# Routing inside the merge, expert rows by indirect DMA, and projections moved into the attention rounds

## The reference, cut to what matters

```python
def moe_swiglu(h, w_router, b_router, w_gate, w_up, w_down):
    t = h.reshape(n_tok, d)                      # 256 tokens x 1024, h = rmsnorm(x)
    logits = t @ w_router + b_router             # 8 experts
    top_v, top_e = lax.top_k(logits, 2)
    gate = jax.nn.softmax(top_v, axis=-1)
    # every token goes to its two experts
    one = (silu(xb @ w_gate[e]) * (xb @ w_up[e])) @ w_down[e]     # 1024 -> 3584 -> 1024
    y = zeros(n_tok, d).at[row_tok].add(out * row_g)

x = x + moe_swiglu(rmsnorm(x, ffn_norm_g[1]), ...)
x = rmsnorm(x, final_norm_g)                     # end of the first block
z = rms_norm(x, pre_mix_norm) @ w_in             # second block, 11 rwkv columns of 128 (r, k, v: 3 each; lora: 2), q, kv, s5
r, k, v, wl, al, gl = split(token_shift(z_rw, mu))
bonus = sum(r * k * r_k, per head) * v           # added to the rwkv output
```

## Time and profile before

| | |
|---|---|
| runs | 2463.23, 2454.6, 2454.49 us; median 2454.6 |
| profiled execution | 2454.6 us, of it span 2452.6 (2.0 around it) |
| mean granted TensorE clock | 0.97 |
| TensorE busy | 2360.8 us, 96% |
| DVE, ACT, POOL busy | 24%, 13%, 6% |
| read from DRAM | 528.09 MB |
| merge's last matmul to the first matmul of expert 0 | 900.36 to 934.41 us |
| eight experts | 934.4 to about 1849 us |
| second block: project, attend | 1865.70 to 1979.90, 1979.90 to 2064.99 us |

### The profile page before, as it was taken

One profiled execution on the slowest core, in us unless ns is written; L12 is line 12 of the kernel. 1 busy time (PEld: TensorE's weight loads), 2 busy tenths in 40 slices (PEclk: granted clock), 3 DMA queues, 4 the chain that ended last, 5 costly groups with the idle time before them and its releaser, 6 DMA issues. The chain is left out here.

```text
span 2452.6 us, 44903 instructions
## 1 busy us (share of the span) xinstructions
PE 2360.8 (96%) x20471; PEld 1590.4 (65%) x20471; DVE 599.1 (24%) x1351; ACT 313.8 (13%) x646; POOL 143.6 (6%) x205
## 2 busy tenths in 40 slices
PE   8999999999999989999999999999998988989998
PEld 7777788888677774535353534444456866668887
DVE  2432220002432121011010110111014265643334
ACT  0222210000231201000000000000001233110002
POOL 1000100000000103000000000000001153300000
PEclk9999999999999988999999999999999967989999
DMA  8322434336322345999999999999994110065330
GB/s 302 136 72 70 168 138 166 143 104 227 132 74 69 137 172 203 386 368 392 388 414 368 412 366 412 368 404 375 380 378 133 62 70 10 1 222 190 110 118 34
DMA packets 165402, 532.02 MB, mean 217 GB/s; under 512 B 16060, under 2 KB 31326, under 8 KB 148830
## 3 DMA queue, kind: packets, MB, share of 16 engines
q1 hardware_dynamic: 153728, 527.76, 57.1%
q10 hardware_dynamic: 11486, 1.41, 0.4%
HBM read 528.09 MB, written 1.05 MB: 216 GB/s over the span
## 5 line engine op out<-in xcount | busy, mean ns | idle before, releaser
L182 PE MATMUL bank<-hT,ring 128*128 128x256 f32 x2720 | 609.1, 382 | 4.3 <-PEq L826 2.8
L182 PE MATMUL bank<-ring,moe_he 128*32 128x512 f32 (+2 forms) x6144 | 577.0, 537 | 0.4 <-DVE moe_he L2008 0.4
L182 PEld LDWEIGHTS bank<-hT,ring 128*128 128x128 f32 x2720 | 514.5, 191 | 83.5 <-issue 13.1
L182 PEld LDWEIGHTS bank<-ring,moe_he 128*32 128x32 f32 x6144 | 199.2, 110 | 373.2 <-issue 371.4
L182 PE MATMUL bank<-ring,moe_actT 128*32 128x256 f32 x5352 | 291.7, 379 | 0.0
L182 PEld LDWEIGHTS bank<-ring,moe_actT 128*32 128x32 f32 x5352 | 173.8, 110 | 116.7 <-issue 3.4
L2062 DVE TENSOR_TENSOR moe_act<-moe_silu,bank 128x512 f32<-128x512 f32 (+2 forms) x48 | 26.8, 614 | 537.5 <-PE bank L182 537.5
L182 PE MATMUL bank<-ring 128*128 128x256 f32 x384 | 86.0, 386 | 6.8 <-DVE ring L631 6.8
L182 PEld LDWEIGHTS bank<-ring 128*128 128x128 f32 x384 | 73.9, 193 | 17.7 <-issue 7.3
L182 PE MATMUL bank<-cffn_act,ring 128*128 128x256 f32 x352 | 79.7, 379 | 0.4 <-DVE cffn_act L1495 0.4
L182 PE MATMUL bank<-ffn_act,ring 128*128 128x256 f32 x352 | 79.4, 379 | 0.0
(11 more groups left out here) (690 smaller groups left out, 2039.8 us busy)
## 6 DMA issues: line engine op xcount, KB each, us to landing
ring<-in_moe_w_down SPq DMA_DIRECT2D x55, 2048.0 KB, 14.3
ring<-in_moe_w_gate SPq DMA_DIRECT2D x32, 2048.0 KB, 16.3
ring<-in_moe_w_up SPq DMA_DIRECT2D x32, 2048.0 KB, 11.0
ring<-in_w_in SPq DMA_DIRECT2D x29, 2048.0 KB, 8.5
ring<-in_moe_w_gate SPq DMA_DIRECT2D x28, 1536.0 KB, 8.9
ring<-in_moe_w_up SPq DMA_DIRECT2D x28, 1536.0 KB, 8.7
ring<-in_w_up SPq DMA_DIRECT2D x10, 2048.0 KB, 9.8
ring<-in_w_out SPq DMA_DIRECT2D x6, 2048.0 KB, 7.9
```

The lines of the kernel that those rows point to most:

```text
L182: ins = pe.matmul(out, lhsT, rhs, start=start, stop=stop, **kw)
```

## The change

**A, early route.** The blocks of `rmsnorm` and `route` are gone. A new `Router` lives in the ring's spare slot. In `merge` of layer 1, after each pair of tiles DVE writes `hT` = `xT`·g (not yet divided by the norm), ACT squares the pair, and TensorE multiplies `hT` by the router's weights and the squares by a column of ones, 32 columns wide (`sums`, four matmuls for a pair, 16 in all). The four column groups are folded by two matmuls, ACT takes the root, DVE forms the logits, and TensorE turns `hT` (16 transposes). At the start of `experts`: ACT copies the turned rows scaled by the norm, DVE picks the experts, TensorE counts positions and gathers for expert 0 as before; a broadcast of the norm scales `hT` for the later use of it. SP writes the token rows to DRAM (`h_rows`, 1 MB) before it issues the experts' slabs.

**B, rows by DMA.** For the experts 1 to 7 the 24 gather matmuls give way to `locate` (2 matmuls, which give each place its token's number), three small DVE operations and three indirect DMAs on POOL's queue (128 rows of 1 KB each), which fetch the rows that DVE then turns into `moe_he`. For the experts 0 to 6 `moe_ye` is written to DRAM by four DMAs on ACT's queue (96 pieces of 1 KB each) and not scattered; during the last expert POOL fetches each token's two rows (four indirect DMAs of 128 rows of 4 KB), DVE weighs and adds them (`weigh`), TensorE turns the sum (`bring`, 16 transposes) and DVE adds it once. Only expert 7 is scattered.

**C, late tiles.** In `project` the v features and the r·k·r_k sums are gone and the three r features stand one by one behind `up`; DVE's and ACT's work follows. In `attend` the three v features follow rounds 1 to 3, the sums and the first s5 feature round 4, the second s5 feature round 5; v is turned after the last round.

```diff
@@ merge, TensorE @@
+            def sums(q):
+                if q == 0:
+                    pe.wait_ge(m.load_in[3], 16)
+                pe.wait_ge(xg_done.sem, 2 * q + 2)
+                pe.wait_ge(sq_done.sem, q + 1)
+                for k in (2 * q, 2 * q + 1):
+                    for c, w, x in ((k % 4, router.w[:, k, :], m.hT), ((k + 2) % 4, router.count, router.sq)):
...
+                if router and q:
+                    sums(q - 1)
-            m.settle(pe, pair_ready)
+                sums(3)
+                pe.wait_ge(added.sem, 2)
+                for j in range(4):
+                    turn(j)
+                pe.wait_ge(part_out.sem, 1)
+                for t in range(TT):
+                    m.mm(pe, m.bank[1][:, 16 * t:16 * t + 9], part_sums[:, t * P:(t + 1) * P], router.fold[:, 0:9], True, True,
+                         tok_ready if t else None)
+                for j in range(4, 2 * KD):
+                    turn(j)
@@ moe @@
-    rmsnorm(m, m.xT[:], m.hT, "ffn_norm_g", 1)
-        route(m, x)
-        experts(m, x, prep)
+        experts(m, x, prep, Router(m), Routes(m, x, c2))
@@ experts, TensorE, for each e @@
                 contract(e, 0)
-                if e:
-                    scatter(e - 1)
                 if e + 1 < N_EXPERTS:
-                    gather(e + 1)
+                    locate(e + 1)
+                if e == LAST:
+                    bring()
                 pe.wait_ge(at_ready.sem, half * e + half)
                 contract(e, 1)
@@ experts, ACT @@
                     if e >= 2:
-                        act.wait_ge(sc_ready.sem, e - 1)
+                        act.wait_ge(written.sem, 64 * (e - 1))
                     act.activation(x.ye[:, 0:2, :], DN[0][:].rearrange("p (g n) -> p g n", g=2), ACT.Copy).then_inc(ye_ready.sem, 1)
+                    act.wait_ge(ye_ready.sem, 2 * e)
+                    for cg in range(4):
+                        act.dma_start(x.y_rows[(e - 1) * CAP:e * CAP, cg * T:(cg + 1) * T].rearrange("(g r) n -> r g n", r=32),
+                                      x.ye[32 * cg:32 * cg + 32]).then_inc(written.sem, 16)
@@ experts, POOL @@
+            for e in range(1, N_EXPERTS):
+                g.wait_ge(index_ready.sem, e)
+                g.wait_ge(he_ready.sem, e)
+                for j in range(GRP):
+                    g.indirect_dma_start(x.picked[:, j, :], None, x.rows_of_h,
+                                         bass.IndirectOffsetOnAxis(ap=x.index[:, e % 2, j:j + 1], axis=0)).then_inc(picked.sem, 16)
+            g.wait_ge(written.sem, 64 * LAST)
+            for t, j, to in ((0, 0, x.h_tok[:, 0, :]), (0, 1, x.second), (1, 0, x.h_tok[:, 1, :]), (1, 1, x.second)):
+                if t and j:
+                    g.wait_ge(weighed.sem, 1)
+                g.indirect_dma_start(to, None, x.y_rows, bass.IndirectOffsetOnAxis(ap=x.pair_row[:, t, j:j + 1], axis=0))\
+                    .then_inc(brought.sem, 16)
@@ project @@
-    ORDER = (("kv", 5), ("r", 3), ("swap", 3), ("k", 3), ("v", 3), ("norm", 3), ("lora", 2), ("q", 3), ("kw", 4), ("up", 9),
-             ("swap_w", 1), ("gates", 9), ("turned", 3))
+    ORDER = (("kv", 5), ("swap", 3), ("k", 3), ("lora", 2), ("norm", 3), ("q", 3), ("kw", 4), ("up", 9), ("r0", 1),
+             ("swap_w", 1), ("gates", 9), ("r1", 1), ("turned", 3), ("r2", 1))
@@ attend, TensorE, after round n @@
+                        if n <= 4:
+                            pe.wait_ge(x_out.sem, 2 * n)
+                        if n <= 3:
+                            project("v", n - 1, m.bank[6][:, 0:T], late_ready)
+                        elif n <= 5:
+                            if n == 5:
+                                pe.wait_ge(late_out.sem, 4)
+                            else:
+                                for p in range(3):
+                                    o = m.bank[7][:, p * T:(p + 1) * T] if p < 2 else m.bank[6][:, T:2 * T]
+                                    pe.matmul(o, m.pair_ones[:], bonus[:, p, :], start=True, stop=True, skip_group_check=True)
+                            project("s5", n - 4, m.bank[6][:, 0:T], late_ready)
```

More of the change, by code:

```diff
@@ L1294, in _ @@
             k = Engine(v, vchain.sem)
+            if router:
+                k.step(v.tensor_reduce(router.fold, m.ident[:].rearrange("p (c n) -> p n c", c=4), AX.X, ALU.add))
             for h in range(2):
@@ L1544, in __init__ @@
         self.iota = sb("iota", [P, CAP])
+        self.picked = spare[:, 2 * D:2 * D + GRP * T].rearrange("p (g n) -> p g n", g=GRP)
+        self.token = spare[:, 2 * D + GRP * T:3 * D].rearrange("p (t n) -> p t n", t=TT)
+        self.diag, self.part = sb("diag", [P, 32]), sb("part", [P, 1])
+        self.found, self.where = sb("found", [P, GRP, 32]), sb("where", [P, GRP, 1])
+        self.index = sb("index", [P, 2, GRP], mybir.dt.uint32)
+        self.rows_of_h = m.nc.dram_tensor("h_rows", [4 * T, T], F32, kind="Internal").ap()
+        self.y_rows = m.nc.dram_tensor("y_rows", [NO_ROW + 1, D], F32, kind="Internal").ap()
+        self.zero, self.row0 = sb("zero", [P, D // P]), sb("row0", [P, 8])
+        self.key, self.held, self.best = (sb(n, [P, TT, 8]) for n in ("key", "held", "best"))
+        self.pair_g = sb("pair_g", [P, TT, 2])
+        self.pair_row = sb("pair_row", [P, TT, 2], mybir.dt.uint32)
+        self.both = sb("both", [P, TT, 2, 8])
+        self.second = spare[:, 2 * D:3 * D]
         self.slot = sb("slot", [P, GRP])
@@ L1828, in experts @@
+def experts(m, x, prep, router, rt):
     nc = m.nc
@@ L1846, in _, with locate @@
         def _(pe):
+            def locate(e):
+                pe.wait_ge(token_ready.sem, 1)
+                pe.wait_ge(sel_ready.sem, e)
+                for t in range(TT):
+                    m.mm(pe, m.bank[4][:, 0:CAP], x.token[:, t, :], x.sel[:, t, :], t == 0, t == TT - 1,
+                         gath if t == TT - 1 else None)
             def gather(e):
-                if e:
-                    pe.wait_ge(sel_ready.sem, e)
                 for g in range(GRP):
@@ L2267, in _ @@
                     m.done_with_slab()
-                    for j in range(3):
-                        feature("r", j * P)
-                    m.done_with_slab()
                     pe.wait_ge(consts.sem, 1)
@@ L2303, in _ @@
                         single(m.pair_ones[:], t1[:, p, :])
-                    for j in range(2):
-                        feature("lora", j * P)
-                    m.done_with_slab()
                     for j in range(3):
@@ L2329, in _ @@
                     ins.then_inc(s_ready.sem, 1)
+                    feature("r", 0)
                     moved(pe, "kw", 2)
@@ L2333, in _ @@
                         single(gsel[:, j, :], gl)
-                    pe.wait_ge(dot_in.sem, 1)
-                    for p in range(3):
-                        ins = pe.matmul(half(6 + p // 2, p % 2), m.pair_ones[:], t2[:, p, :], start=True, stop=True)
-                    ins.then_inc(dot_ready.sem, 1)
+                    feature("r", P)
                     pe.wait_ge(p_ready.sem, 1)
```

502 lines of the change are left out of this document (324 added, 178 removed).

## The result

The changed kernel takes 2435.5 us (median of 5 runs, 2427.7 to 2437.5) against 2454.5 before (5 runs, 2447.3 to 2463.2): ratio 0.990, 95% interval 0.988 to 0.993. The forecast was 2399 with a range of 2388 to 2424. The direction was right, the size was not: 19 us of 56.

A forecast was written before the change was run, and what follows sets the result against it. TensorE, busy for 96% of the span, was taken as the bound, with the DMA engines' weight stream close behind in the experts. 2454.6 - 18.2 (A) - 34.0 (B) - 3.6 (C) = 2398.8, said as 2399 us, range 2388 to 2424.

The forecast's parts named there:

- A: Out-projection's end to first expert: 34.05 us go and 15.9 come back, giving -18.2 us, between -15 and -20.5.
- B, TensorE's side: Experts: scatters and gathers leave TensorE, `locate` and 16 transposes come; -34.0 us if nothing new is waited for.
- B, the new wait: Experts, second contract wave: three row fetches take 11 us of the 13 left, so they fit with 2 to spare.
- The first rival: Experts: fetched rows come later than 13 us, TensorE waits 2 to 3 us in each of 7 experts; 2415, chance 0.22.
- B, DMA's side: Experts' weight stream: weights and new bytes take 107.6 us against a period of 108.85, so it just fits, no stall.
- the second rival: Experts: weights become the bound, waits for slabs grow from expert to expert; 2412, between 2403 and 2429, chance 0.13.
- C, project: Second block's `project`: six features leave ahead of `up` (-21 us), its tail grows from 20.5 to 29; -12.5 us.
- C, attend: Second block's `attend`: three features 10.5 us, sums 1.5, waits about 1.5, less 4.7 taken back; +8.9 us.
- The term for the clock: `attend`: filled waits and a fuller TensorE keeping the high clock longer, taken as -4.7 us, bounds 0 and about -9.
- the third ("no clock gained"): Second block or route gives less (longer DVE chain, no clock gained, first gather at low clock); +9 us, 2408, chance 0.06.

The follow-up runs named there:

- no_fetch: The changed kernel without the indirect fetches of the rows of experts 1 to 7, which work on zeros; executed once, 2416.5 us.
- early_locate: `shift_later` with `locate` and the fetch moved earlier, into `expand` (experts 1 to 6) or ahead of the first contract wave (expert 0); 2407.3 us, again 2407.4.
- fetch_pool: `shift_later` with the experts' fetches as plain DMAs of fixed rows on POOL's queue, not indirect ones of chosen rows; executed once, 2419.8 us.
- shift_later: The changed kernel with DVE's token shift of a late v feature moved into the next round, behind the first softmax preparation; 2409.0 us, again 2423.

## Why the prediction was off

**A** was right. The forecast's 15.9 us have two lots of `sums` ahead of the projection's last quarter in them; these took 0.57 each, so with the 15.4 behind the out-projection it is 16.5. The third lot, the add, the square and the last lot took 2.2, where 2.7 was forecast; the gather 5.1, just above my upper end of 4.9. The whole stretch was 16.3 us shorter in the profiled execution and 17.4 in most others, against -18.2.

**B, TensorE's side.** The step that failed is "B gives -34.0, if nothing new is waited for": it took what is not waited for as free. Of the 34.0 us `no_fetch` gives 31.4; `locate` at 0.62 instead of 0.3 makes seven times 0.32, 2.2 us, which all but closes the account. The rest, 7.5 to 10 us, comes with the fetches: a hole of up to 1.2 us an expert with the indirect DMAs, a cost on an engine that has no part in them. No row of the kernel before shows such a DMA, and I had bounded only its landing, not a side effect. The 7.5 to 10 are not all to be had by closing the hole, since about 4 us then turn into waits for weights.

**B, the new wait.** Right in the time: 7.0 us for one fetch, 10.2 for the chain of three against 11, and no wait. The working behind the 11 was in part luck: it counted 384 packets, and the trace has 144 for the three. By the Trainium skill, page "DMA: Bandwidth & Descriptors", section "Anatomy of one DMA — SWDGE (gpsimd) path", one of them would take an estimated 2.3 us. The trace shows 7.0 beside the weights, and 10.2 for the three against the 6.9 by that figure. The first rival (2415) was real only on ACT's queue.

**B, DMA's side.** No stall was forecast and there is none in the changed kernel, but at a period of 110.7, not the 108.9 for which it was worked out. At 109.2 the waits appear, 3.2 to 4.5 us, all in expert 7 (`early_locate`, `fetch_pool`); without the fetches' bytes they don't (`no_fetch`). So the second rival was near: its mechanism, a wait for slabs, is there as soon as TensorE runs at nearly the forecast's pace.

**C, project**: -11.5 and -12.3 against -12.5. The sum is right with some luck: in the profiled execution the scores behind `up` start 22.3 us earlier where 21 was taken, and the tail from there takes 31.3 us where 29 was taken and 31 named as the limit.

**C, attend** is the step that failed most. I priced three features, the sums and "about 1.5 of waits" and took back 4.7 for the clock. For B I asked what is queued behind a new wait; for C I did not: the wait of DVE for ACT's copy of the late feature stands ahead of the divisions of the next round. It is on DVE's list in the code. The term for the clock had the wrong sign: the sum took back 4.7 for a fuller TensorE, and the clock was lower (mean 0.72 against 0.80). The reading behind it, that the clock falls wherever TensorE waits, was too simple: in `shift_later` TensorE waits three times for 0.6 us in the rounds with the clock at 1.00. It was also sized by a row that was not wholly at the low clock: the 5.26 of the earlier trace rows has a granted clock of 0.69 around it (2004 to 2010). The waits cost 5.5 us and the clock 17, by the profiles of `shift_later` at its lower level; at its higher level moving the call brings 10 us, so 12.5 of the 17 can be lost again without these waits, for a reason that stays open. None of the rivals named it; the third ("no clock gained") was priced at 9 us, not at 21.

With the call moved, the executions at the lower level of `shift_later` and `early_locate` lie 45 to 53 us under the kernel before, of the 55.8 forecast; those at the higher level lie 32 to 35 under it.

## What to carry to other kernels

For every wait that a change adds to an engine, write down the next instruction of that engine that another engine needs, in every part of the change; here one such wait made C a loss of 13 to 16 us, and moving the call by half a round made it a gain in five of nine executions. Where TensorE runs small matmuls between waits, look at the granted clock of what follows a new wait: here waits of 5.5 us stood ahead of up to 17 us of slower rows. When a stream of weights runs at a share of 1.01, ask what comes back as a wait for weights: here about 4 of 7.8 us. Where executions fall into two levels, compare all of them and not two medians.

## What the runs showed of the hardware

- With three indirect DMAs on POOL's queue (128 rows of 1 KB each) in it, TensorE's second contract wave took 15.7 to 16.8 us instead of 15.56, with no semaphore between the matmuls; with plain DMAs of the same size on the same queue, of fixed rows, it took 15.56 each time.
- Beside a full stream of weights (share 1.0) such a DMA lands in 7.0 us from POOL's queue and the plain one in 7.1, in 48 packets each; from ACT's queue the plain one has 144 packets and lands in 11.1.
- The same attention code ran in 92.3 us at a mean granted clock of 0.87 and in 104.9 at 0.76, with the same waits.
